# Dilated projections as seven products of quarters, with the combination's rows kept in DRAM

## What is computed

```python
proj = hn @ w_in
u_f, g_f, q, k, v, g_a = split(proj)          # q, k, v: 24 heads of 64
q = rms_norm(q, q_norm_w) * HEAD_DIM ** -0.5
k = rms_norm(k, k_norm_w)
for c, (window, dilation) in enumerate(((128, 1), (512, 4), (2048, 16))):
    o_c, lse_c = dilated_window_attention(q[c], k[c], v[c], window, dilation)
alpha = softmax(stack(lses), axis=0)
y_a = sum(alpha * outs) * silu(g_a)
h = h + concat([y_f, y_a]) @ w_out
```

## Time and profile before

| what | value |
|---|---|
| median of three runs | 3931.61 us (3929.72 to 3931.7) |
| the profiled execution's own time | 3927.89 us |
| its span, first to last instruction | 3926.1 us |
| TensorE busy | 3600.2 us, 92% |
| ScalarE, VectorE, GpSimd busy | 1198.7, 982.7, 442.4 us |
| mean granted TensorE clock | 0.963 |

### The profile page before, as it was taken

The page is one execution under the profiler, slowest core; times in us unless marked ns, Lnnn a source line. Parts: engine busy times, 40 slices in busy tenths (PEclk is TensorE's granted clock), DMA queues, the critical chain, the costliest instruction groups (busy, mean ns, idle before and its releaser), DMA issues. The chain is left out here.

```text
span 3926.1 us, 43246 instructions
## 1 busy us (share of the span) xinstructions
PE 3600.2 (92%) x16895; PEld 1933.6 (49%) x16895; DVE 982.7 (25%) x2410; ACT 1198.7 (31%) x2525; POOL 442.4 (11%) x337
## 2 busy tenths in 40 slices
PE   6389898979799999999899999999999999799899
PEld 3148384847444545544354445544454545344444
DVE  3323324232321212344122112221122212111132
ACT  3213131221331323323233445355444445211000
POOL 0100101020200000053000020003000300030143
PEclk9699898989899999999999999999999999999999
DMA  6110010000301011232140475326534423432221
GB/s 220 21 35 26 23 28 23 18 27 22 92 17 30 22 30 20 75 93 91 45 17 12 17 57 17 6 17 62 12 12 14 60 17 12 36 92 72 96 91 70
DMA packets 296873, 171.50 MB, mean 44 GB/s; under 512 B 162601, under 2 KB 263480, under 8 KB 293690
## 3 DMA queue, kind: packets, MB, share of 16 engines
q1 hardware_dynamic: 290406, 158.27, 26.8%
q10 hardware_dynamic: 6272, 10.49, 0.8%
HBM read 147.03 MB, written 21.70 MB: 43 GB/s over the span
## 5 line engine op out<-in xcount | busy, mean ns | idle before, releaser
L2035 PE MATMUL d<-hT,w 128*128 128x512 f32 x2560 | 1123.0, 594 | 8.2 <-POOL qk_w L2025 8.2
L2035 PEld LDWEIGHTS d<-hT,w 128*128 128x128 f32 x2560 | 485.4, 190 | 612.9 <-issue 602.9
L989 PE MATMUL n<-hT,wo 128*128 128x512 f32 x1024 | 455.4, 603 | 22.1 <-issue 11.7
L563 PE MATMUL m<-hT,w 128*128 128x512 f32 x768 | 339.4, 605 | 35.4 <-PEq L473 19.1
L989 PEld LDWEIGHTS n<-hT,wo 128*128 128x128 f32 x1024 | 195.1, 193 | 262.0 <-issue 249.9
L563 PEld LDWEIGHTS m<-hT,w 128*128 128x128 f32 x768 | 149.0, 195 | 223.9 <-issue 223.9
L2503 PE MATMUL f<-hT,w 128*128 128x512 f32 x512 | 223.0, 596 | 20.5 <-PEq L76 16.5
L568 PEld LDWEIGHTS m<-w,hT 128*128 128x128 f32 x2048 | 229.3, 192 | 1.9 <-issue 1.9
L568 PE MATMUL m<-w,hT 128*128 128x128 f32 x2048 | 229.3, 275 | 0.0
L2238 DVE CUSTOM_DVE_ANT_0 sneg<-d,bias 128x192 f32<-128x192 f32 (+1 forms) x384 | 109.7, 324 | 351.5 <-PE d L2069 341.6
L2198 ACT ACTIVATE sq<-d 128x512 f32<-128x512 f32 x96 | 57.2, 596 | 413.4 <-PE d L2035 413.4
(11 more groups left out here) (319 smaller groups left out, 4049.8 us busy)
## 6 DMA issues: line engine op xcount, KB each, us to landing
w<-in_w_in SPq DMA_DIRECT2D x68, 512.0 KB, 3.8
trig<-in_trig SPq DMA_DIRECT2D x16, 1024.0 KB, 4.9
ada<-in_w_ada SPq DMA_DIRECT2D x6, 2048.0 KB, 18.6
xg<-in_x ACTq DMA_DIRECT2D x4, 2048.0 KB, 23.6
rb<-r_rows SPq DMA_DIRECT2D x16, 512.0 KB, 5.6
wo<-in_w_in SPq DMA_DIRECT2D x16, 512.0 KB, 3.8
mix_ml<-in_x SPq DMA_DIRECT2D x16, 512.0 KB, 3.6
x<-mix_ml SPq DMA_DIRECT2D x16, 512.0 KB, 2.9
```

What stands on the lines that cost most here:

```text
L563: last = nc.tensor.matmul(bank[n % 2][:], w[:, s % O_, k], hT[:, k, (n % 4) * TB:(n % 4 + 1) * TB], start=(k == 0), stop=(k == KC - 1))
L989: last = nc.tensor.matmul(bank[b][:], w[:, s, k], hT[:, k, tb * TB:(tb + 1) * TB], start=(k == 0), stop=(k == KC - 1))
L2035: last = nc.tensor.matmul(bank[tb][:], w[:, s, k], hT[:, k, tb * TB:(tb + 1) * TB], start=(k == 0), stop=(k == KC - 1))
```

## The change

Keys and queries of a unit, and values with another unit's values or with the gate, are projected as one pair n of two slabs (20 pairs). A pair is computed in two halves j of 1024 rows each as a 2x2 block product with seven instead of eight products of quarters: a quarter is four of the eight contraction pieces, 512 rows, 128 columns. GpSimd makes four mixed weight tiles per pair (`make`), the sums of hT's blocks are made once, ahead (`first_sums`, `last_sums`; hT's quarter is restored at the end). A half yields four blocks x, y, z, u in SBUF: ScalarE copies two products out of PSUM (`hold`), VectorE adds five (`add`), GpSimd joins two (`join`). Squares and norms then read these blocks instead of PSUM. The units come in the order of dilation 4, 16, 1; the last has keys and queries alone, and its values, made with the first unit's, wait in DRAM, as do gate, outputs o of the first two units and the combined rows. The combination goes in eight pieces of 256 rows through two buffers (`fetch_piece`, `combine`, `keep_piece`). `root` is as before but for one wait. The core of the diff (`...` where lines are left out):

```diff
+class SevenProducts:
+    STEPS = 7
+    BANKS = 4
...
+    def load(self, sp, t, n, i):
+        if n > 0:
+            sp.wait_ge(self.made, 4 * n)
+            if i != 1:
+                sp.wait_ge(self.prod, 14 * (n - 1) + self.STEPS + {0: 1, 2: 3, 3: 6}[i])
...
+    def make(self, nc, pool, n):
...
+        nc.gpsimd.tensor_tensor(mixed[:, 0], raw[:, 1], raw[:, 0], ALU.subtract).then_inc(self.made, 1)
+        pool.wait_ge(self.raw_in[3], 16 * (n + 1))
+        pool.wait_ge(self.made, 4 * n + 1)
+        nc.gpsimd.tensor_tensor(mixed[:, 1], raw[:, 3], mixed[:, 0], ALU.subtract).then_inc(self.made, 1)
...
+    def product(self, nc, pe, bank, n, j, i):
...
+        if i == 1:
+            need(pe, self.held, 2 * s)
+        elif i == 5:
+            pe.wait_ge(self.held, 2 * s + 1)
+        else:
+            need(pe, self.full, 5 * s + {2: -2, 3: -1, 4: 0, 6: 1, 7: 2}[i])
+        for k in range(h):
+            last = nc.tensor.matmul(bank[self.bank_of(n, j, i)][:], w[:, k], x[k], start=(k == 0), stop=(k == h - 1))
...
+    def join(self, nc, pool, n, j, what):
+        s = 2 * n + j
+        u = self.u[:, j]
+        if what == 1:
+            pool.wait_ge(self.full, 5 * s + 1)
+            pool.wait_ge(self.held, 2 * s + 2)
+            nc.gpsimd.tensor_tensor(self.z[:], u, self.y[:], ALU.add).then_inc(self.pooled, 1)
+        else:
+            pool.wait_ge(self.full, 5 * s + 3)
+            nc.gpsimd.tensor_tensor(self.y[:], u, self.y[:], ALU.add).then_inc(self.pooled, 1)
 class Combine:
+    PIECES = 8
+    NQ = T // 8
...
+    def fetch_piece(self, sp, t, g, m):
+        half, NQ, i = P // 2, self.NQ, m % 2
+        cols = slice(m * NQ, (m + 1) * NQ)
+        n = self.PIECES * g + m
+        if m >= 2:
+            if g < PAIRS - 1:
+                sp.wait_ge(self.kept[i], 16 * (n // 2))
+            else:
+                sp.wait_ge(self.mixed, n - 1)
         for h in range(2):
+            rows = slice(h * half, (h + 1) * half)
+            sp.dma_start(self.alpha[i][rows], t["alpha"][g, :, h, cols].partition_broadcast(half)).then_inc(self.piece_in[i], 16)
+        sp.dma_start(self.others[i], t["o_rows"][g].rearrange("c p n -> p c n")[:, :, cols]).then_inc(self.piece_in[i], 16)
+        sp.dma_start(self.gate[i], t["g_rows"][g][:, cols]).then_inc(self.piece_in[i], 16)
...
+    def keep_piece(self, sp, t, g, m):
+        sp.wait_ge(self.mixed, self.PIECES * g + m + 1)
+        sp.dma_start(t["att_rows"][g][:, m * self.NQ:(m + 1) * self.NQ], self.gate[m % 2]).then_inc(self.kept[m % 2], 16)
```

SyncE's list for a pair, from its start, and GpSimd's whole list:

```diff
+                    load(n + 1, 1)
+                    if g > 0:
+                        store_stats(a - 1)
+                    fetch_bias(g)
+                    if g > 0:
+                        late.fetch_stats(sp, t, g - 1)
+                    load(n + 1, 0, 2, 3)
+                    if g > 0:
+                        late.store_alpha(sp, t, g - 1)
...
+                        late.fetch_piece(sp, t, g - 1, 0)
+                        late.fetch_piece(sp, t, g - 1, 1)
+                    load(n + 2, 1)
+                    if g > 0:
+                        for m in range(2, 5):
+                            late.keep_piece(sp, t, g - 1, m - 2)
+                            late.fetch_piece(sp, t, g - 1, m)
+                    store_block(n + 1, 0, t["v_rows"][g])
...
+                for n in range(5 * PAIRS):
+                    g, p = divmod(n, 5)
+                    for j in range(2):
+                        if n > 0 or j > 0:
+                            join(n, j, 1)
+                            join(n, j, 2)
+                        if g > 0 and p == 0 and j == 0:
+                            late.factors_pool(nc, pool, g - 1)
+                        if g > 0 and p == 1 and j == 0:
+                            for m in range(3, 8):
+                                late.combine(nc, pool, g - 1, m)
+                            pool.wait_ge(late.kept[1], 16 * late.PIECES // 2 * g)
+                            nc.gpsimd.memset(prob, 0.0).then_inc(zeroed, 1)
+                    if n + 1 < 5 * PAIRS:
+                        seven.make(nc, pool, n + 1)
+                    if g > 0 and p == 0:
+                        pool.wait_ge(out, NB * N_CFG * g)
+                        for m in range(3):
+                            late.combine(nc, pool, g - 1, m)
```

TensorE's order in a unit, and ScalarE's in the key projection:

```diff
+                def project_keys(a):
+                    n = keys_of(a)
+                    for j in range(2):
+                        for i in range(1, 8):
+                            project(n, j, i)
+                            if j == 0 and i <= 3:
+                                tail(a - 1, i - 1)
+                            if j == 1 and i == 1:
+                                sums(a, 3)
+                            if i == 4:
+                                sums(a, 4 * j)
+                            elif i == 6:
+                                sums(a, 4 * j + 1)
+                            elif i == 7:
+                                sums(a, 4 * j + 2)
...
+                        square(a, 4 * j)
+                        hold(n, j, 4)
+                        root(a, 4 * j)
+                        square(a, 4 * j + 1)
+                        root(a, 4 * j + 1)
+                        square(a, 4 * j + 2)
+                        root(a, 4 * j + 2)
```

In the Fourier stage, for g = 0:

```diff
+                        late.fetch_stats(sp, t, last_pair)
+                        late.store_alpha(sp, t, last_pair)
+                        for m in range(4):
+                            late.fetch_piece(sp, t, last_pair, m)
+                        for m in range(last_pair):
+                            sp.dma_start(mix_att[:, m], t["att_rows"][m]).then_inc(late.att_in, 16)
...
+                        if g == 0:
+                            for m in range(4 + 2 * s, 6 + 2 * s):
+                                late.fetch_piece(sp, t, last_pair, m)
...
                     for k in range(NTR, KH):
                         fetch_trig(g, k)
```

More of the change, by code:

```diff
@@ L1786, in __init__ @@
         self.rows = sb("mix_f", [P, PAIRS, T])
-        self.o = self.rows[:, 1:4]
-        self.w = sb("w6", [P, 4, KC, P])
-        self.alpha = sb("alpha6", [P, N_CFG, TB])
+        self.o = self.rows[:, 1]
+        piece = [self.rows[:, 2 + i, 0:6 * self.NQ].rearrange("p (m n) -> p m n", n=self.NQ) for i in range(2)]
+        self.alpha = [p[:, 0:3] for p in piece]
+        self.others = [p[:, 3:5] for p in piece]
+        self.gate = [p[:, 5] for p in piece]
         self.stat = sb("stat6", [P, 2, N_CFG, U])
@@ L2031, in _, with sums @@
+                seven.restore(nc, pool, 5 * PAIRS)
             @block.tensor
             def _(pe):
-                def chain(s, tb):
-                    for k in range(KC):
-                        last = nc.tensor.matmul(bank[tb][:], w[:, s, k], hT[:, k, tb * TB:(tb + 1) * TB], start=(k == 0), stop=(k == KC - 1))
-                    last.then_inc(proj, 1)
-                def sums(a, n):
-                    pe.wait_ge(squared, 8 * a + n + 1)
-                    if n == 0:
+                def sums(a, e):
+                    pe.wait_ge(squared, 8 * a + e + 1)
+                    if e == 0:
@@ L2141, in _, with project_values, attend @@
+                def project_values(a):
+                    n = keys_of(a) + 1
+                    for j in range(2):
+                        for i in range(1, 8):
+                            project(n, j, i)
+                            if j == 0 and i == 1:
+                                sums(a, 7)
+                def attend(a):
                     scores(a, 0)
-                    need(pe, out, NB * a)
-                    need(pe, rooted, 8 * a + 8)
+                    if cfg(a) == 0:
+                        sums(a, 7)
@@ new lines, in project_keys @@
+                def project_keys(a):
+                    n, g = keys_of(a), a // N_CFG
+                    for j in range(2):
+                        if j == 1:
+                            square(a, 3)
+                        hold(n, j, 1)
+                        if j == 0 and a > 0:
+                            copies(a - 1, NB - 2)
+                            copies(a - 1, NB - 1)
+                        if j == 1:
+                            root(a, 3)
+                            if g > 0 and a % N_CFG == 0:
+                                late.factors_act(nc, act, g - 1)
+                        square(a, 4 * j)
[5 more added lines that the diff above has]
+                        root(a, 4 * j + 2)
@@ new lines, in project_values @@
+                def project_values(a):
+                    n, g = keys_of(a) + 1, a // N_CFG
+                    for j in range(2):
+                        s = 2 * n + j
+                        if j == 0:
+                            square(a, 7)
+                        hold(n, j, 1)
+                        if j == 0:
+                            root(a, 7)
+                        hold(n, j, 4)
```

(28 more changed lines are left out.)

609 lines of the change are left out of this document (395 added, 214 removed).

## The result

The changed kernel takes 3976.5 us (median of 4 runs, 3968.5 to 3979.4) where the kernel before takes 3930.7 on the same chip: the medians are 45.8 us apart. I had forecast 3909 us, 23 us faster on the profiled execution, and a range that ends at 3952.

A forecast was written before the change was run, and what follows sets the result against it. TensorE was taken to bound the dilated stage. Products -137.4, sum waits -2.3, A +20, B +18, C +51 and +5, E +20.6, small terms +2 gave -23 us on the profiled execution: 3909 us, range 3862 to 3952.

The forecast's parts named there:

- term A: Root chain with table loads inside the shorter product steps of the dilated stage: sums stall, +20 us (0 to 45).
- B: Undilated units: root 7 runs at the head of the attention instead of under a value projection, +18 us (0 to 25).
- Term E: Last pair, combined in the Fourier stage: fourth trig tile queues behind all eight pieces, +19 us and 1.6 for the clock.
- Small terms: Last unit's statistics +1, first sums and loads +1; value copies, row stores and turning v 0 (turning at most 14).
- term C: Combination through DRAM in eight pieces delays scores: 17 us for each of three pairs, +51, and +5 for the clock.
- Piece transfers are slow: Rival: the combination's piece landings exceed 9 us; 3942 us at 9.5, 3949 at 10; chance 0.20.
- Handoffs and port: Rival: 24 norms between sums 0 and 1 grow by 1.07 us beside GpSimd, 26 us, 3935; chance 0.16.
- The combination hides: Rival: with 5 us landings the last piece comes 9 us sooner per pair, 3866 to 3850 us; chance 0.14.
- The loads are not there: Rival: both functions of a root in one table, A goes and B nearly, 3871 us; chance 0.04.

The follow-up runs named there:

- run 1: Changed kernel with the combination of the first three pairs left out (factors, piece fetches, weighing, piece stores): 0.9860 of the time of the kernel before.
- run 2: Changed kernel with weighed pieces written over the unit's own rows and stored from there behind the next fetch: 0.9998 of the time of the kernel before.
- run 9: Changed kernel with pieces of the first three pairs fetched without the weights, 384 of 768 KB left out: 0.9882 of the time of the kernel before.
- run 12: Changed kernel, first three pairs' weight transfers reading 192 different rows instead of three rows 64 times, same bytes: 0.9941 of the time of the kernel before.
- run 3: Changed kernel with ScalarE given one table set for logarithm and exponential after each half's gate activations: 0.9994 of the time of the kernel before.

## Why the prediction was wrong, and where it was right

**Right.** TensorE bound the stage, and 137.4 us of products went. A check from the other side: the single gains of no combination, one table and the tile are 98 + 45 + 29 = 172 us; 172 less the 43 measured leaves 129 us of saving, my sum without those terms was 138, and the 129 is known to some 10 us. The table loads cost about what terms A and B say together (38 us; 45 measured), though that is partly luck: both terms counted waits alone, and some 20 of the 45 are clock. Sums waited 23.5 us, of them 7.5 for root 7 in the four undilated units, which leaves 16 for the 20 of term A; most pieces are 0.3 to 0.8 us, as forecast, but three are 1.1, 2.1 and 3.5. B alone was rather too high: an undilated attention grew by 3 to 4 us beside its two sums, not 4.5. Term E was 19 + 1.6; the wait is 21.7 and the stage lost 23.3. Small terms: turning v cost 32.7 us instead of 26.2; I took 0, of at most 14.

**Wrong: term C, 51 + 5 us where 98 were measured.** Its mechanism was the one described (pieces 3 to 7 and a memset ahead of the joins, three idles, VectorE's add and a join last). The step that failed is "Writing a piece and waiting for it: 2.4 us, as alpha's store", and beside it "I take that" for a landing of 7.3 us. The store of the earlier trace rows had no fetch in front of it: the issue before it stands 11 us earlier. In the change each store is issued right behind the other buffer's fetch and completes after it: 5.7 us. The landing was 8.1 to 9.1. A round was therefore 18.7 us instead of 14.1 (7.3 + 4.4 + 2.4). Counted from the start of the keys, piece 7 was weighed at 136.9 us, not at 120: 5.2 us of that had gone before piece 0 (its fetch was issued at 62.1 for 58.3 and landed 1.4 us slower), 11.7 between piece 0 and piece 7 (61.7 us for 50: three rounds of 4.6 us more, less 2.2 because piece 1 came 5.1 us behind piece 0 and not 7.3). The products ahead of the scores ended 3.8 us later too, so the first idle, 30.6 us, is 12.5 us over the 18.1 that I had (scores at 128.4, the last product done at 110.3). Runs 1, 2 and 9 show the parts.

**Beneath it, one cause.** Both numbers are inflated by the same transfer, the weights read by 64 partitions from the same rows (run 12). The profile of before held the sign, and I read it as "twice the 4.0 us of 512 KB" for 768 KB and took it for a matter of bytes. Each of these transfers, issued four together, was slow already:
```profile
alpha<-alpha SPq DMA_DIRECT2D x20, 384.0 KB, 6.2
```
That is 6.2 us for three quarters of the bytes that w brought in 4.0. Unshared pieces were used 4.9 to 5.6 us behind their fetch (run 12).

**The clock.** I took 1.6 us for each of three idles; run 1 makes it some 4.5. TensorE's groups grew by 7.6 (products, against the full clock), 6.4 (sums), 6.4 (scores), 3.3 and 3.1 us (turns, values), 27 us, and run 3 takes 17 of these away with waits that were none longer than 3.5 us. So more of the clock is lost on many short waits, where term A had counted only the waits themselves, than on the three long idles (13 us, run 1).

**The rivals.** "Piece transfers are slow" is what happened, given 0.20; with landings of 8.6 us alone it would have meant 3928, though, for it did not see that a store queued behind a slow fetch is slow as well. "Handoffs and port" showed little: VectorE's norms take 1.01 to 1.31 us in the mean for 0.99, 13 us over 96 of them and not 26 over 24, and sums waited for an add in one place, 0.8 us. "The combination hides" had landings near 5 us; run 12 made such landings, and idles of some 10 us stayed even so (9.95 and 10.51 in two pairs). "The loads are not there" was wrong, 80 pairs were.

## What to carry to other kernels

Read a transfer's time from the queue it will stand in: a store behind a fetch completes with the fetch, and a wait on it puts both in the loop. Give a result its own place, so that the next fetch waits only for the reader.

Look at microseconds per byte for each kind of transfer before pricing a larger number of them; a broadcast from few DRAM rows can be twice as slow as the same bytes from separate rows (6.0 us for 3.3 here), and it need not be (512 KB from one row in 4.7). When steps get shorter, ask what they covered: table loads that cost at most 7 us beside 6.9 us cost 45 us beside 3.4, and keeping both functions in one set is a line.

A saving on the bound engine can be real and buried. Here some 129 us were, under three waits that stood in the order of a queue or of a table, and all three could be cut down without touching the seven products.

## What the hardware showed that I had not expected

- 192 KB read as three rows by 64 partitions: 6.0 us; 192 KB from 192 rows of the same length: 3.3 us; the fetch and the store behind them are slow or fast with them (6.3 and 5.6 us, against 3.3 and 2.0). One row of 4 KB read by 128 partitions: 512 KB in 4.7 us.
- The granted clock fell behind a wait as short as 2.10 us (0.68 over the next products, which took 5.28 us for 3.60), and a turn took 1.98 us behind 3.17 us of idle as behind 30.64.
